# Four layers on one core: the mixers' 512-column products split into three fast products, with GpSimd making the low parts of the weights

## What is computed

```python
# each of the four layers (the branches differ between the two blocks)
u = rmsnorm(x, g) @ w_in                         # 1024 x 7964, or x 6048
y = [branch_n(slices of u) for n in range(4)]
gates = sigmoid(u[..., -4096:])                  # 4 branches x 1024 columns
merged = sum(gates[n] * (y[n] @ w_branch[n]) for n in range(4))
x = x + merged @ w_out                           # second block: x + rmsnorm(merged @ w_out)
h = rmsnorm(x, g_ffn)
x = x + (silu(h @ w1) * (h @ w3)) @ w2           # layer 1: the best 2 of 8 experts
```

## Time and profile before

| | |
|---|---|
| median of 3 runs | 2905.73 us (2905.04 to 2906.57) |
| span of the profiled execution | 2898.2 us |
| TensorE busy | 2674.2 us, 92% |
| VectorE, ScalarE, GpSimd busy | 50%, 39%, 1% |
| mixers' stage of layer 1, with router | 600 to 1000 us |
| experts | 1000 to 1871 us |
| mixers' stage of layer 2 | 1871 to 2179 us |

### The profile page before, as it was taken

How to read it: one execution, slowest core, us unless ns; L and a number is a source line. 1 busy time by engine, 2 the same in 40 slices (tenths; PEclk the granted TensorE clock), 3 DMA queues, 4 the chain that set the end, 5 groups by cost and what they waited for, 6 DMA issues and landing times.

```text
span 2898.2 us, 29276 instructions
## 1 busy us (share of the span) xinstructions
PE 2674.2 (92%) x10791; PEld 1885.8 (65%) x10791; DVE 1454.0 (50%) x2219; ACT 1137.3 (39%) x1487; POOL 33.4 (1%) x64
## 2 busy tenths in 40 slices
PE   6999789989997799999999999799989979999897
PEld 5754458876644477787787787565537866554786
DVE  2224435523244288898898888521225542121554
ACT  1211134411111177787787777412114431211443
POOL 2000000000000000000000000000000000000000
PEclk9999899999998799999999999899999989999899
DMA  6323265434232299999999999542355533334551
GB/s 211 135 98 116 73 218 174 148 111 157 73 116 73 92 367 318 330 355 315 322 342 335 318 333 348 174 134 99 123 185 180 174 105 113 116 131 150 174 201 41
DMA packets 373238, 549.25 MB, mean 190 GB/s; under 512 B 20828, under 2 KB 273104, under 8 KB 373024
## 3 DMA queue, kind: packets, MB, share of 16 engines
q1 hardware_dynamic: 369072, 535.82, 53.9%
q0 software_dynamic: 3648, 9.87, 1.3%
q10 hardware_dynamic: 432, 2.37, 0.2%
HBM read 546.98 MB, written 1.05 MB: 189 GB/s over the span
## 4 chain that ended last, share of the span: by engine, by line
PE 70%; DVE 5%; ACT 2%; issue 2%; DMA 0%; SPq 0%; ACTq 0%; DVEq 0%
PE pb L676 19%; PE mb L869 11%; PE mb L871 11%; PE mb L870 11%; PE pb L671 3%; PE pb L999 2%; PE pb L869 1%; PE pb L871 1%; PE pb L870 1%; DVE w_lo L1987 1%; PE pb L661 1%; PE pb L713 1%; PE mb L1019 1%; PE mb L953 1%; PE mb L1021 1%
## 5 line engine op out<-in xcount | busy, mean ns | idle before, releaser
L1987 DVE TENSOR_TENSOR w_lo<-ring,w_hi 128x1024 fp32r<-128x1024 f32 x726 | 871.1, 1223 | 272.7 <-ACT w_hi L1336 211.9
L676 PE MATMUL pb<-ring,hT 128*128 128x512 f32 (+3 forms) x1856 | 763.3, 570 | 11.4 <-ACT hT L1220 6.6
L676 PEld LDWEIGHTS pb<-ring,hT 128*128 128x128 f32 x1856 | 358.0, 196 | 380.6 <-issue 362.8
L1373 ACT ACTIVATE w_hi<-ring 128x1024 fp32r<-128x1024 f32 x528 | 557.9, 1063 | 79.9 <-PE mb L871 74.4
L869 PE MATMUL mb<-w_hi,hT_hi 128*128 128x512 f32 x1232 | 495.6, 402 | 18.5 <-DVE hT_lo L1987 9.1
L871 PE MATMUL mb<-w_lo,hT_hi 128*128 128x512 f32 x1232 | 483.8, 393 | 0.0
L870 PE MATMUL mb<-w_hi,hT_lo 128*128 128x512 f32 x1232 | 482.7, 392 | 0.0
L1336 ACT ACTIVATE w_hi<-ring 128x1024 fp32r<-128x1024 f32 x198 | 208.7, 1060 | 203.7 <-PE mb L871 152.2
L869 PEld LDWEIGHTS mb<-w_hi,hT_hi 128*128 128x128 f32 x1232 | 233.4, 189 | 73.6 <-issue 15.0
L871 PEld LDWEIGHTS mb<-w_lo,hT_hi 128*128 128x128 f32 x1232 | 232.9, 189 | 50.8
L870 PEld LDWEIGHTS mb<-w_hi,hT_lo 128*128 128x128 f32 x1232 | 233.7, 190 | 45.4
(11 more groups left out here) (392 smaller groups left out, 2249.8 us busy)
## 6 DMA issues: line engine op xcount, KB each, us to landing
ring<-in_moe_w SPq DMA_DIRECT2D x264, 1024.0 KB, 9.0
ring<-in_w_in SPq DMA_DIRECT2D x48, 2048.0 KB, 7.8
ring<-in_ffn_w SPq DMA_DIRECT2D x33, 1024.0 KB, 7.8
ring<-in_w_ffn_gate SPq DMA_DIRECT2D x22, 1024.0 KB, 5.2
ring<-in_w_ffn_up SPq DMA_DIRECT2D x22, 1024.0 KB, 7.8
ring<-in_w_ffn_down SPq DMA_DIRECT2D x22, 1024.0 KB, 9.8
ring<-in_w_out SPq DMA_DIRECT2D x8, 2048.0 KB, 7.9
ring<-in_w_branch SPq DMA_DIRECT2D x8, 1024.0 KB, 4.8
```

The costliest lines, as they stand in the source:

```text
L676: ins = mm(bank[:, 0:m], hT[:, k, i * P:(i + 1) * P], wv[:, k, col - chunk_lo:col - chunk_lo + m], start=k == 0, stop=k == KD - 1)
L1373: f(w_hi[:, n % NPIECE], ring[:, c % NSLOT, q * PIECE:(q + 1) * PIECE], ACT.Copy).then_inc(e_hi_ready, 1)
L1987: return tt(dst, src, hi.bitcast(F32), ALU.subtract)
```

## The change

In all four layers the products whose weights come 512 columns wide and whose tokens are the stationary operand become split products: the last two chunks of `w_in` in layers 0 and 1, the second chunk in layers 2 and 3, all gates and the output product. They are 24 banks (8 matmuls each) in layers 0 and 1 and 22 in layers 2 and 3. The other chunks, the branch products and the experts' arithmetic stay.

For these, ScalarE makes the high parts of 48 or 44 pieces a layer (`high_to`, placed between its other work), GpSimd makes the low parts, a new duty (`low_parts` in its program), and `hT` and the turned `merged` get high and low parts too. Two banks (both token tiles) are filled together, piece by piece (`split_jobs`); where one gate bank stood between small products, half of two banks (two pieces) now stands.

Memory for this comes from the ring, which has two narrower slots; a third slot for the feed-forward and the down weights (`third_gu`, `down_w`) lie where the mixers' buffers are. In layers 0 and 1 chunks 4 and 5 change places. The first four pieces of a feed-forward are made later on VectorE. ScalarE's first exponential of the gated linear attention stands ahead of the gates of branch 2, behind them before.

```diff
-SLOTW = KD * 2 * FC + 2 * D
+SLOTW = KD * 528
...
+    (MO, 264, [("tok", 0, MO, 264), ("tok", 1, MO, 264)]),
     (SDT, 516, [("ch", ((GQ, 128), (GK, 128))), ("tok2", 0), ("tok2", 1)]),
-    (MO, 264, [("tok", 0, MO, 264), ("tok", 1, MO, 264)]),
...
-        ring = sb("ring", [P, NSLOT, SLOTW])
+        ring = sb("ring", [P, 2, SLOTW])
...
+        third_gu = sb("third_gu", [P, GU_W])
+        down_w = sb("down_w", [P, NSLOT, DN_W])
...
+            def low_parts(lo, hi):
+
+                for m in range(lo, hi):
+                    pool.wait_ge(w_hi_ready, m + 1)
+                    nc.gpsimd.tensor_tensor(w_lo[:, m % NPIECE], source[m][0], w_hi[:, m % NPIECE].bitcast(F32),
+                                            ALU.subtract).then_inc(pool_split, 1)
...
+            def split_jobs(L, key, qs):
+
+                B = BK[L]
+                for q in qs:
+                    m = PC.of[(L,) + key + (q,)]
+                    if q == 0:
+                        for i in range(T):
+                            open_bank(B, key + (i,))
+                    pe.wait_ge(*low_done(m))
+                    for i in range(T):
+                        it = slice(i * P, (i + 1) * P)
+                        bank = pb[B.index[key + (i,)] % 4]
+                        for kk in range(2):
+                            k = 2 * q + kk
+                            ins = split_product(bank[:], hT_hi[:, k, it], hT_lo(k)[:, it], m, slice(kk * 512, (kk + 1) * 512),
+                                                k == 0, k == KD - 1)
+                        if q == 3:
+                            ins.then_inc(filled, 1)
+                    if q < 3:
+                        ins.then_inc(w_used, 1)
...
-            def gate(L, b, h, i):
-                w = weights((L, "gate", b, h))
-                proj_job(BK[L], ("gate", b, h, i), w, 0, 512, ("tok", i, 0, 512))
+            def gate(L, b, h, half):
+                split_jobs(L, ("gate", b, h), (2 * half, 2 * half + 1))
...
+            def merged_turned(L):
+                B = BK[L]
+                for q in range(4):
+                    job = ("turn", 4 + q)
+                    act.wait_ge(filled, B.filled(job))
+                    f(hT_hi[:, 2 * q:2 * q + 2].rearrange("p k s -> p (k s)"), pb[B.index[job] % 4][:], ACT.Copy).then_inc(mT_hi_ready, 1)
...
                 mixers(L)
-                if L == 0:
-                    low_parts(0, 0, NPIECE)
+                merged_low(L)
                 add_out(L)
                 if L == 0:
                     scale_by_gain(1)
+                    low_parts(0, 0, NPIECE)
                     ffn(0)
```

More of the change, by code:

```diff
@@ L180, in bank_jobs2, with split_items1, split_items2, __init__ @@
     return jobs
+def split_items1():
+    items = [("proj", 6), ("proj", 7)]
+    items += [("gate", b, h) for b in range(NBR) for h in range(2)]
+    return items + [("wout", h) for h in range(2)]
+def split_items2():
+    items = [("proj", 1)]
+    items += [("gate", b, h) for b in range(NBR) for h in range(2)]
+    return items + [("wout", h) for h in range(2)]
+class Pieces:
+    def __init__(self):
+        self.n, self.maker, self.of = 0, [], {}
+    def add(self, key, count, maker):
+        for q in range(count):
+            self.of[key + (q,)] = self.n
+            self.maker.append(maker)
+            self.n += 1
+    def nth(self, m):
+        return self.maker[:m + 1].count(self.maker[m])
 class Banks:
@@ L187, in __init__ @@
         self.jobs = jobs
-        self.by = ["dve" if j[0] in ("merge", "wout") else "act" for j in jobs]
+        self.by = ["dve" if j[0] in ("merge", "wout") or (j[0] == "turn" and 4 <= j[1] < 8) else "act" for j in jobs]
         n_act, n_dve = self.by.count("act"), self.by.count("dve")
@@ L404, in build, with low_done, place_used, ring_slot @@
             base = BK[-1].end
-        items, find = [], {}
-        uses = [0] * NSLOT
-        def add_item(key, loads, free):
-            s = sum(i != "experts" for i in items) % NSLOT
+        PC = Pieces()
+        MIX, FFN = [0] * 4, [0] * 3
+        for L in range(4):
+            MIX[L] = PC.n
+            for key in (split_items1() if L < 2 else split_items2()):
+                PC.add((L,) + key, 4, "pool")
+            if L != 1:
+                u = (0, None, 1, 2)[L]
+                FFN[u] = PC.n
+                PC.add(("ffn", u), ALL_PIECES, "dve")
+        def low_done(m):
+            return (w_split if PC.maker[m] == "dve" else pool_split), PC.nth(m)
+        closing = {}
+        n_used, used_at = 0, {}
+        for key, m in PC.of.items():
+            if key[0] != "ffn" and key[-1] == 3:
+                L, job = key[0], key[1:-1]
+                closing[m] = BK[L].filled(job + (1,))
+            else:
+                n_used += 1
+                used_at[m] = n_used
+        def place_used(m):
+            return (filled, closing[m]) if m in closing else (w_used, used_at[m])
+        items, find, source = [], {}, {}
+        uses = [0] * NSLOT
+        turn_of = [0]
+        def ring_slot():
+            s = turn_of[0] % 2
+            turn_of[0] += 1
+            return s
+        def add_item(key, s, loads, free):
             uses[s] += 16 * len(loads)
@@ new lines, in ffn_items @@
+                last = (pieces(c + 1) if c < NF else ALL_PIECES) - 1
+                add_item(("ffn", u, c), s, loads, low_done(FFN[u] + last))
+                for n, (pc, q) in enumerate(PIECE_LIST):
+                    if pc == c:
+                        src = gu_slot(s)[:, q * PIECE:(q + 1) * PIECE] if q < GU_PIECES else (
+                            down_w[:, s, (q - GU_PIECES) * PIECE:(q - GU_PIECES + 1) * PIECE])
+                        source[FFN[u] + n] = (src, find[("ffn", u, c)] if n == pieces(c) else None)
@@ L744, in mixers @@
                 ins.then_inc(alpha_mm, 1)
-                chunk(L, 6)
-                chunk(L, 7)
+                pe.wait_ge(hT_mix_split, 4 * L + 4)
+                split_jobs(L, ("proj", 6), range(4))
+                split_jobs(L, ("proj", 7), range(4))
                 pe.wait_ge(soft_ready, L + 1)
@@ L1266, in gate @@
                     act.wait_ge(dve_emptied, B.emptied(("merge", b - 2, 1, 1))[1])
[L1267 removed]
+                for i in range(T):
+                    job = ("gate", b, h, i)
+                    empty(B, job, (gates[:, b % 2, i, h * 512:(h + 1) * 512], pb[B.index[job] % 4][:], ACT.Sigmoid, 1.0))
             def yturned(L, b):
```

413 lines of the change are left out of this document (246 added, 167 removed).

## The result

The changed kernel takes 2886.73 us (median of 4 runs, 2880.49 to 2893.30) against 2905.61 us of the kernel before on the same chip (2905.04 to 2906.57): ratio 0.9937, 95% interval 0.9925 to 0.9949. So it is faster, by 19 us, where 93 were forecast; 2886.73 lies above the range of 2773 to 2868. The profiled execution took 2887.1 us, its span is 2885.3.

What follows compares the result with a forecast made beforehand. TensorE's work was taken as the bound, plus its waits for VectorE. Terms of -137 (matmuls), +19 (new order) and +25 (GpSimd beside VectorE) summed to -93 us, forecasting 2813 us, range 2773 to 2868.

Steps and rivals of the forecast that it cites:

- GpSimd beside VectorE: Low parts holding VectorE chains that TensorE waits for: 10 chains, up to 50 us, half taken, 25 us.
- all handoffs: Pieces late because ScalarE stands at the exponentials, two places a layer: 0 to 30 us, 8 taken.
- Main term: Replacing 736 plain 512-column matmuls by three split ones each saves 0.186 us apiece, in all 137 us.
- slow stretches don't change the sign: At the lower clock split matmuls take 0.43 us, close to double, as plain ones would, so replacing still saves.
- New order: Costs of transfers, proj 7, gated attention, turned `merged`, feed-forward starts and handoffs across the layers: 19 us.
- The first feed-forward's start: In layer 0, two high parts and two low parts delay TensorE's start to 404.7, +3.8 us.
- GpSimd's duration: A low part of 1024 columns on GpSimd, estimated from its fills, takes 2.65 us.
- GpSimd is not the bound: In layer 1, pieces are needed every 5.2 us once matmuls are faster, against 2.65 us a low part.
- the rival that the engines exclude each other: All ten VectorE chains meet two low parts, costing 50 us, for 2837 us; chance 0.25.
- The rival of whole waits for each instruction: VectorE sets layers 0 and 1's pace from mean wait 0.54 us; no gain at 0.8, 3000 us at 1.0; chance 0.08.
- My own signs of being wrong: Low parts over 4 us, layer 1 VectorE busy or idle up over 50 us, or transfers ending TensorE's gate waits.
- should not change: The feed-forward streams and the experts' passes were to stay as before in the profile after.

Runs made afterwards that it cites:

- e13: Changed kernel with GpSimd's low parts over 32 columns (the rest zeros), 480 bytes free ahead of `fhT_hi`, and attention copies first: 2772.77 us.
- e7: Changed kernel where, in layers 2 and 3, ScalarE copies the turned attention output before the output product's first four high parts: 2868.94 us.
- e1: Changed kernel with GpSimd's low parts over 32 of 1024 columns, the mixers' other low parts left as zeros: 2817.05 us.
- e2: Changed kernel with GpSimd's low part replaced by fills of the same tile, about as long, which read nothing: 2835.80 us.
- e4: Changed kernel with the first four high parts of layers 2 and 3 made after the turned input's copies, GpSimd's small loads ahead of its low parts: 2867.16 us.
- e9: Changed kernel with 480 bytes left free ahead of `fhT_hi`, so tiles begin at the same place modulo 2048 bytes: 2865.52 us.
- e15: Changed kernel with e4, e7 and e9, VectorE's low parts for proj 6 and 7 in layers 0 and 1, GpSimd's in two 512-column instructions: 2811.82 us.
- e10: Kernel before the change with 1568 bytes left free ahead of `hT_lo`: 2935.46 us, ratio 1.0108.
- e6: Changed kernel with only the memory layout altered, `w_hi`, `w_lo` and `hT_hi` placed behind the mixers' memory: 2895.04 us.

## Why the prediction was wrong

The step that failed first is "GpSimd beside VectorE": it took 25 us, and the hold measured about 50. That alone would give 2838 us, inside the range. The rest is what the sum put at nothing or nearly so: the length of a low part (about 20), the places of the tiles in memory (21) and the copies behind ScalarE's high parts (18, where all handoffs had 8).

- **Main term, 137 us: right.** The output product of layer 1 starts at 936.32 and its last matmul at 958.02 or just after, 22 us in place of 27.7, and the matmuls there are 0.2272 us apart. The mixers of e13 are 32.2, 32.3, 29.2 and 30.7 us shorter than before, where 36, 36, 33 and 33 less the order's costs were forecast. That "slow stretches don't change the sign" is right too, but their size changed, and the sum had no term for it (the clock, below).
- **New order, 19 us: near in its sum, wrong in its place.** With the three causes away (e13), the gain is 133 us in the medians, 15 more than the 118 of the main term and this one; so if the main term is exact, the order and whatever else is left cost about 4 us in place of 19, with the copies (18) taken out by e7. The first feed-forward's start costs 3.8 to 4.0 us by TensorE's idle time, where 3.8 was forecast. The handoffs (8 of 0 to 30) were looked for at the exponentials; they were in layers 2 and 3, at the attention copies, and worth 18 us (e7). I had read where ScalarE waits, not what it waits for while somebody else needs its next instruction.
- **GpSimd's duration: right** (2.43 us for 2.65), and "GpSimd is not the bound" too: it works 102.6 of 243 us in the middle of layer 1. Its length still costs about 20 us (e1 against e2): as I read it, the slot in the ring comes free later and a piece is late by 2.4 us wherever TensorE has no other work, but no run tells these two apart. The sum had no term for it outside the handoffs.
- **GpSimd beside VectorE, 25 us: it measured about 50**, the upper bound, with the cause of the rival that the engines exclude each other. But the rival's count was wrong: ten chains that meet two low parts. The trace shows some twenty held instructions in each of layers 0 and 1, 42 us a layer, and nine in layer 2, 15 us (83.3 us of VectorE against 67.9 in e1). TensorE has other work for more than half of that, so the price came out near the bound by another way than the bound was made: that the two agree is luck. And the norms of layers 2 and 3 stood in no count of mine as a place where all is on the path: 8.5 and 9.9 us (table), both back in e4. The rival of whole waits for each instruction is right in mechanism and wrong in size: w = 41 us more in the middle of layer 1 by 231 instructions is 0.18 us, far from the 0.54 from which it would decide, since GpSimd works 42% of the time and many instructions have an operand in PSUM. My own signs of being wrong didn't fire either: VectorE's busy time in layer 1's mixers grew by 47 us, just under the 50 that I had named.
- **The experts' passes and the feed-forwards "should not change": wrong, 21 us** (e9). The diff moved tiles in memory and I priced moves at nothing.

The accounts: 2813 of the forecast, less its 25, plus 70 (GpSimd), 21 (tiles' places) and 18 (copies) give 2897; the other terms came out up to 15 us below their sum, which gives 2882, and 2887 was measured. These prices hold what the clock takes. Over the span it fell from 0.957 to 0.940: by the trace TensorE works for 230 us at the lower level (1.2 GHz), 153 before, and half of the difference, 38 us, is lost by that (an estimate, since busy time has modelled ends). It closes the account of TensorE's busy time, which fell by 73 us and not by 137: 73, the 38 and e9's 21 (busy 2579.4 us in place of 2600.9) make 132. In e13 the work at the lower level is 176 us. So waits of TensorE cost more than their own length, a quarter of e1's 66 us and more than half of what e7 gained in layer 3. No run changed the clock alone, so that the waits are what lowers it is argued from their going together, not shown.

## What to carry to other kernels

Before work goes to GpSimd, list the chains of short VectorE instructions that TensorE waits for and where the new work lands in time: each of them will wait for one whole GpSimd instruction, so place that work elsewhere or cut it small (the first alone got 20 us in e4, both together some 13 more in e15). Read a wait's price together with the granted clock of its stage, since removing a wait can give back more than its length (e7). When a diff moves tiles in memory, compare the places of the stationary and the moving operands before and after, and look at the distance of matmul starts in stages that the change doesn't touch. In an engine that works in order, ask of each wait what stands behind it (e7 again).

## What the runs showed of the hardware

- A matmul (128x512, float32r, at full clock) costs 0.227 us when the tile of the next stationary operand and the moving tile begin at the same place modulo 2048 bytes, and on average 0.233 (`fhT_hi`, `fhT_lo`) to 0.238 (`xg_lo` next) when the stationary tile stands 480 bytes below the moving one (the changed kernel, against e9). With 1568 bytes above it (e10) the same pairs take as long, and that is the same distance if places repeat every 2048 bytes. The Trainium skill ("SBUF — State Buffer", Who interferes with whom) says that TensorE's two reads are independent and that it never waits on anyone; in these runs the distance depends on the places of the two, by 2% of an expert's pass. Only these offsets and e6's were tried, so the modulus itself stays open, and so does the cause.
- A strict alternation: VectorE with two SBUF inputs or a `TENSOR_SCALAR` and GpSimd's subtraction take turns, instruction by instruction (2.27 us for 0.16 us of work); instructions with an input in PSUM (`gates<-pb,gates` 0.69 us in all nine cases that start during a subtraction) and `TENSOR_REDUCE` (0.69) kept their lengths. The long `RECIPROCAL` (1.85 us) never met a subtraction, so it says nothing.
- GpSimd's fill of 128x1024 takes 0.957 us, its subtraction 2.43, one of 512 columns 1.34, of 32 columns 0.29; waits are in these means.
